# Moving where the second block's TensorE operands begin in SBUF: weight slots 8 and 16 bytes, the other buffers 128 bytes off the 256-byte lines

## The chip, the cores and the metric

The kernel runs on one core of a Trainium2 chip. The metric is the device time of one execution in microseconds (us): 2687.53 us before the change, the median of 3 runs (2683.39 to 2690.18). TensorE multiplies a moving operand, streamed from SBUF (the on-chip memory with 128 partitions), by a stationary operand that a weight load has put into the array; results go to PSUM. The other engines are VectorE (DVE), ScalarE (ACT), GpSimd (POOL) and SyncE (SP), which issues most DMAs.

## The reference, cut to what matters

Two transformer blocks run one after the other on 512 tokens of width 1024. The first block has two layers of attention and a mixture of experts; the change does not touch its arithmetic. The second block has two layers of this form:

```
h    = rms_norm_2(x, norm_mix_pre[l])
proj = h @ w_in[l]                          # 1024 -> 12 slices of 256
mix  = concat(conformer, stick-breaking attention, retention, short conv) @ w_out[l]
x    = x + rms_norm_2(mix, norm_mix_post[l])
f    = conv_ffn(rms_norm_2(x, norm_ffn_pre[l]), ffn_up[l], ffn_conv_w[l], ffn_down[l])
                                            # 1024 -> 2 x 2816, conv, silu(gate) * up, 2816 -> 1024
x    = x + rms_norm_2(f, norm_ffn_post[l])
```

All inputs are float32.

## The kernel before

In the second block every large product is made of three matmuls (`split_matmul`, lines 240 to 242): both operands are held as a high part and a low part in the type fp32r, and hi x hi, hi x lo and lo x hi are summed in one PSUM bank. Their lines in the profile are L240, L241 and L242. In a profile row `ps<-A,B` of these lines A is the moving operand and B the stationary one.

Weights come in pieces of 1 MB (128 partitions x 2048 float32): 12 pieces of `w_in`, 4 of `w_out`, 22 of `ffn_up` and 11 of `ffn_down` in each layer. SP loads a piece into one of two `raw` buffers; ACT copies it to the high part of a slot of `ring` (L2637), DVE subtracts to make the low part (L2892), and TensorE waits for `lo_made` before it uses the slot. Most pieces use the two slots `in_w` of the tile `w`; the first two pieces of `w_in` use `first`, two of `w_out` use `outs`, the second piece of `ffn_up` uses `second_up`, and `ffn_down` takes `in_w` and the halves of `h` (`in_h`) in turn, and `last_down` for its last piece.

Which operand moves depends on the product. For `w_in` and `ffn_up` the activations `h` move (512 columns, or 256 where the tokens are done in halves, `in_halves`) and the weights are stationary (128 columns); for the value slices of `w_in` it is the other way round, 256 columns of weights moving. For `w_out` and `ffn_down` 512 columns of weights move, and the mixer's outputs `y` or the feed-forward activations `act` are stationary.

Addresses: a tile `gap` before `h` makes `h`, and with it `w` and all that the planner `plan` lays behind them, begin at a multiple of 256 bytes (`LINE`). `plan.put` takes an offset in KB. So before the change `h`, both slots of `w`, `first`, `outs`, `last_down`, `act` and the `y` tiles all begin at a multiple of 256 bytes. `second_up` (at 76.3125 KB) begins 64 bytes past one. In the first block, the tile `lat_d` (1280 columns as 8 rows of 160 float32, 640 bytes apart) begins at multiples of 256 bytes and 128 past them in turn, row by row. A reader needs these three facts below.

`SECOND_AT` is where the plan of the second block's opening (`open1`, with the slots `first`) begins; it has to agree with `plan.at` (the assertion before `first = cl.split`).

The order of work on every engine is written out by hand and waits on semaphores.

Of the kernel before, what the change touches and what calls it, by code (L numbers as in the profile page):

```python
# [15 lines left out]
F32R = mybir.dt.float32r  # L16
# [4 lines left out]
P = 128  # L21
SEQ = 512
D = 1024
NT = SEQ // P
ND = D // P
# [98 lines left out]
LINE = 256  # L124


def gap_to_line(at):

    return -(-(-at // 32) * 32) % LINE
# [1293 lines left out]
    st.retire(k)  # L1423


SECOND_AT = 83 * 1024 + 768


DOWN_CUTS = (0, 256, 512, B_QR + B_KVR + B_ROPE)
# [679 lines left out]
def second_block(k, cl):  # L2109

    st = Stage(k.nc, "l")
# [1 line left out]
    par, eps, ln_eps = st.sb("par", [P, DEPTH, 3, P]), st.sb("eps", [P, 1]), st.sb("ln_eps", [P, 1])  # L2113
    ss, sd, rs = (st.sb(n, [P, 5, 2, NT]) for n in ("ss", "sd", "rs"))
    st.sb("gap", [P, gap_to_line(k.nc.sbuf_base)], mybir.dt.uint8)
    h, w = Split(st, "h", [P, ND, SEQ]), Split(st, "w", [P, 2, 2048])
    plan = Plan(k, "l", k.nc.sbuf_base)
    assert plan.at % LINE == 0

    z = [plan.put(f"z{n}", 5 * n, [P, TRI]) for n in range(2)]  # L2120
    ln1 = [plan.put(f"ln{n}", 10 + 5 * n, [P, TRI]) for n in range(2)]
# [30 lines left out]
    cm = AfterMix(st, plan, "c", 0, 84)  # L2152
    cl.lend(st, cm)

    in_w = [(w.hi[:, n, :], w.lo[:, n, :]) for n in range(2)]
    in_h = [tuple(y[:, 4 * n:4 * n + 4, :].rearrange("p a s -> p (a s)") for y in (h.hi, h.lo)) for n in range(2)]
    ring = [tuple(y[:, :] for y in x) for x in first] + [in_w[n % 2] for n in range(2, N_SLICES)]
    ring += [tuple(y[:, :] for y in x) for x in outs] + in_w
# [989 lines left out]
def program(nc, a, out):  # L3148
    k = Core(nc, a, out)
    routes = [Routes(nc, f"r{layer}") for layer in range(DEPTH)]  # L3150
    first = Stage(nc, "first")
    gap = gap_to_line(nc.sbuf_base)
    if gap:
        nc.alloc_sbuf_tensor("shared_gap", [P, gap], mybir.dt.uint8)
    base = nc.sbuf_base
    assert base % LINE == 0
    k.attention_buffers(first)
    weights = ExpertWeights(k, first)
    openings = [Collect(k, Plan(k, "open0", base), routes[0], 0, (112, 120, 128, 136), 96, 170, ((32, 40), (48, 56))),
                Collect(k, Plan(k, "open1", base + SECOND_AT), routes[1], 1, (36, 44, 68, 76), 24, 0, ((8, 52), (16, 60)))]  # L3160

    def held_first(sp):
        weights.load(sp, 0, 2, 2, lambda c: None, range(1, 2))
        weights.load_ahead(sp, 0)

    def held_second(sp):
        weights.load(sp, 1, 1, 1, lambda c: None, range(5, 6))
        weights.load_ahead(sp, 1)

    rt = window_layer(k, base, 0, routes[0], weights)  # L3170
    experts(k, 0, routes[0], rt, weights, lambda n: down_piece(k, n), held_first, openings[0])
    rt = latent_layer(k, base, 1, openings[0], routes[1], weights)
    experts(k, 1, routes[1], rt, weights, lambda n: in_piece(k, 0, n), held_second, openings[1])
    first.retire(k)
    second_block(k, openings[1])
# [24 lines left out]
```

## Time and profile before

| what | value |
|---|---|
| median of 3 runs | 2687.53 us |
| the profiled execution | 2690.91 us |
| its span, first to last instruction | 2689.1 us |
| granted TensorE clock, mean over the span | 0.974 of full speed |
| PE busy | 2505.2 us, 93% of the span |
| DVE, ACT, POOL busy | 1077.2, 754.3, 181.6 us |
| second block, from about 1496 us | granted clock 1.00, DMA share 0 to 0.47 by stage |

The second block begins at about 1496 us: its first split product starts there. A matmul's duration in the profile (0.39 us for 512 columns) contains the way through the array and overlaps the next one, so what a stream of matmuls costs is read from the distance between two starts, here called the spacing.

### The profile page before, as it was taken

To read this page: it belongs to the slowest core of one execution; us is meant where nothing else is said; L and a number is where in the kernel's file an instruction comes from. 1 tells how busy PE (TensorE), PEld (TensorE's weight loads), DVE (VectorE), ACT (ScalarE), POOL (GpSimd) and SP (SyncE) were. 2 spreads that over 40 slices of the span, in tenths; PEclk is the share of its full clock that TensorE was granted. 3 is DMA by queue.
4 is the path that set the end of the run, shared out by engine and by line. 5 is a ranking of instruction groups with operands and counts; after the bars stand their busy time and mean duration, and the time that the engine had idled before them with its cause. 6 is when DMAs were issued, how large, how long until landed. Compare 5 with 4: busy or idle time off the path is not lost.

```text
span 2689.1 us, 36859 instructions
## 1 busy us (share of the span) xinstructions
PE 2505.2 (93%) x14582; PEld 1853.1 (69%) x14582; DVE 1077.2 (40%) x1628; ACT 754.3 (28%) x1221; POOL 181.6 (7%) x302
## 2 busy tenths in 40 slices
PE   8997999888899979998888999999999999999999
PEld 7675666544576656665454777888888877888887
DVE  4753011100445541110001666655543666555542
ACT  3530000000245410000001353443332454433431
POOL 0001111111000001111111010000000010000000
PEclk9997999999999989999999999999999999999999
DMA  5339999999622189999998312223232212222231
GB/s 174 84 144 368 414 414 416 419 414 411 257 94 79 40 342 411 411 412 415 417 419 340 139 63 86 83 91 101 94 126 94 102 56 99 81 93 95 94 125 55
DMA packets 175401, 576.56 MB, mean 214 GB/s; under 512 B 20560, under 2 KB 104080, under 8 KB 125618
## 3 DMA queue, kind: packets, MB, share of 16 engines
q1 hardware_dynamic: 164722, 558.07, 53.8%
q0 software_dynamic: 10560, 16.81, 1.8%
q8 instruction: 86, 1.41, 0.2%
q14 instruction: 33, 0.27, 0.0%
HBM read 569.56 MB, written 23.07 MB: 220 GB/s over the span
## 4 chain that ended last, share of the span: by engine, by line
PE 62%; SPq 19%; DMA 3%; DVE 3%; issue 3%; ACT 2%; DVEq 0%; POOLq 0%; ACTq 0%
PE ps L240 14%; PE ps L242 14%; PE ps L241 14%; SPq L1183 13%; SPq L1189 6%; PE ps L1333 6%; PE ps L1351 4%; DMA first_weights<-in_moe_w_up 2%; PE ps L1303 1%; ACT lat_probs L1841 1%; PE ps L1650 1%; PE ps L2340 1%; PE ps L1666 1%; PE ps L2376 1%; DMA open_rows<-r_y 1%
## 5 line engine op out<-in xcount | busy, mean ns | idle before, releaser
L240 PE MATMUL ps<-l_h_hi,l_w_hi 128*128 128x512 f32 x896 | 352.9, 394 | 0.0
L241 PE MATMUL ps<-l_h_lo,l_w_hi 128*128 128x512 f32 x896 | 348.8, 389 | 0.0
L242 PE MATMUL ps<-l_h_hi,l_w_lo 128*128 128x512 f32 x896 | 348.7, 389 | 0.0
L1333 PE MATMUL ps<-first_weights,moe_xsT 128*64 128x256 f32 x2688 | 309.5, 380 | 39.6 <-DMA first_weights<-in_moe_w_up 26.9
L1412 DVE TENSOR_TENSOR moe_hid<-moe_silu,ps 128x256 f32<-128x256 f32 x64 | 27.0, 421 | 767.9 <-PE ps L1333 767.9
L1333 PEld LDWEIGHTS ps<-first_weights,moe_xsT 128*64 128x64 f32 x2688 | 225.8, 137 | 132.9 <-issue 82.7
L2892 DVE TENSOR_TENSOR l_w_lo<-l_raw,l_w_hi 128x2048 fp32r<-128x2048 f32 x76 | 174.0, 2292 | 270.1 <-ACT l_w_hi L2637 269.9
L1385 ACT ACTIVATE moe_ys<-ps 128x512 f32<-128x512 f32 x64 | 38.2, 597 | 672.3 <-PE ps L1351 672.3
L1351 PE MATMUL ps<-first_weights,moe_hidT 128*64 128x512 f32 x672 | 177.2, 675 | 38.3 <-DVE moe_hidT L1414 38.3
L2637 ACT ACTIVATE l_w_hi<-l_raw 128x2048 fp32r<-128x2048 f32 x76 | 145.2, 1914 | 179.8 <-PE ps L242 168.9
L240 PEld LDWEIGHTS ps<-l_h_hi,l_w_hi 128*128 128x128 f32 x896 | 168.2, 188 | 37.5 <-issue 2.9
L241 PEld LDWEIGHTS ps<-l_h_lo,l_w_hi 128*128 128x128 f32 x896 | 168.2, 188 | 35.4 <-issue 1.4
L242 PEld LDWEIGHTS ps<-l_h_hi,l_w_lo 128*128 128x128 f32 x896 | 168.2, 188 | 35.4
L1333 PE MATMUL ps<-first_ring,moe_xsT 128*64 128x256 f32 x1344 | 160.8, 392 | 18.4 <-DMA first_ring<-in_moe_w_up 10.0
L1333 PEld LDWEIGHTS ps<-first_ring,moe_xsT 128*64 128x64 f32 x1344 | 115.3, 141 | 67.1 <-issue 41.5
L1351 PEld LDWEIGHTS ps<-first_weights,moe_hidT 128*64 128x64 f32 x672 | 60.2, 152 | 126.3 <-issue 126.3
L1351 PE MATMUL ps<-first_ring,moe_hidT 128*64 128x512 f32 x352 | 88.9, 650 | 20.1 <-DVE moe_hidT L1414 20.1
L1291 POOL DMA_INDIRECT r_y<-moe_ys,moe_put x64 | 65.4, 1022 | 297.4 <-ACT moe_ys L1385 280.2
L1382 ACT ACTIVATE moe_silu<-ps 128x256 f32<-128x256 f32 x64 | 24.6, 384 | 214.3 <-PE ps L1333 214.3
L2956 DVE SCALAR_TENSOR_TENSOR l_gate<-l_glu,l_par,l_gate 128x512 f32<-128x512 f32 x120 | 81.8, 752 | 0.1
L240 PE MATMUL ps<-l_w_hi,l_act_hi 128*128 128x512 f32 x192 | 74.9, 390 | 0.0
L241 PE MATMUL ps<-l_w_lo,l_act_hi 128*128 128x512 f32 x192 | 74.7, 389 | 0.0
(589 smaller groups left out, 4304.2 us busy)
## 6 DMA issues: line engine op xcount, KB each, us to landing
first_weights<-in_moe_w_up SPq DMA_DIRECT2D x84, 1024.0 KB, 27.9
first_weights<-in_moe_w_down SPq DMA_DIRECT2D x84, 1024.0 KB, 27.7
first_weights<-in_moe_w_gate SPq DMA_DIRECT2D x84, 1024.0 KB, 27.4
first_ring<-in_moe_w_up SPq DMA_DIRECT2D x44, 1024.0 KB, 27.5
first_ring<-in_moe_w_down SPq DMA_DIRECT2D x44, 1024.0 KB, 27.6
l_raw<-in_ffn_up SPq DMA_DIRECT2D x44, 1024.0 KB, 5.0
first_ring<-in_moe_w_gate SPq DMA_DIRECT2D x40, 1024.0 KB, 27.6
l_raw<-in_w_in SPq DMA_DIRECT2D x22, 1024.0 KB, 4.9
```

What stands on the lines that cost most here:

```text
L240: pe.matmul(out, stationary[0], moving[0], start=first, stop=False)
L241: pe.matmul(out, stationary[0], moving[1], start=False, stop=False)
L242: return pe.matmul(out, stationary[1], moving[0], start=False, stop=last)
L1183: sp.dma_start(self.gate_up[s][m][:, 4 * c:4 * c + 4, :].rearrange("p j c -> p (j c)"), a[name][layer, e, c * 512:(c + 1) * 512, :].rearra ...
L1189: sp.dma_start(self.down[s][:, 2 * c:2 * c + 2, :].rearrange("p j c -> p (j c)"), a["moe_w_down"][layer, e, c * 256:(c + 1) * 256, :].rear ...
L1291: pool.indirect_dma_start(out=r.y_dram, out_offset=bass.IndirectOffsetOnAxis(ap=put[:, 0:1], axis=0), in_=ys[:, :], in_offset=None, bounds ...
L1333: ins = pe.matmul(k.ps[64 * h:64 * h + 64, 2 + m, 0:256], xsT[:, j, :], piece[:, j % 4, 256 * h:256 * h + 256], start=j == 0, stop=j == ND ...
L1351: ins = pe.matmul(k.ps[64 * h:64 * h + 64, 4, :], hidT[:, j % 2, 64 * (j // 2):64 * (j // 2) + 64], weights.down[s][:, j, 512 * h:512 * h ...
L1385: act.activation(ys[:, :], k.ps[:, 4, :], ACT.Copy).then_inc(ys_kept, 1)
L2637: act.activation(ring[n][0], piece(m), ACT.Copy).then_inc(hi_made, 1)
L2892: dve.tensor_tensor(lo, piece(m), hi.bitcast(F32), ALU.subtract).then_inc(lo_made, 1)
L2956: ins = dve.scalar_tensor_tensor(acc, glu[:, i, c:c + SEQ], par[:, l, 2, 2 * c + i:2 * c + i + 1], acc, ALU.mult, ALU.add)
```

## The change

Three edits. The two halves of `w` are no longer tiles of their own but views into one tile that is 128 bytes longer: slot 0 begins 2 float32 (8 bytes) past the start, slot 1 begins 4096 + 4 float32 past it (16 bytes past a multiple of 256); the low part of each begins 2048 float32 behind its high part, so it has the same 8 or 16 bytes. Because `w` is 128 bytes longer, everything in `plan` begins 128 bytes later, and so does `SECOND_AT`: `first`, `outs`, `last_down`, `act` and the `y` tiles now begin 128 bytes past a multiple of 256, and `second_up` 192. The assertion on `plan.at` goes. `h` stays where it was. The instructions of every engine, their order and their waits stay as they are; only addresses differ.

```
-SECOND_AT = 83 * 1024 + 768
+SECOND_AT = 83 * 1024 + 768 + 128
...
     st.sb("gap", [P, gap_to_line(k.nc.sbuf_base)], mybir.dt.uint8)
-    h, w = Split(st, "h", [P, ND, SEQ]), Split(st, "w", [P, 2, 2048])
+    h, w = Split(st, "h", [P, ND, SEQ]), st.sb("w", [P, 4 * 2048 + 32], F32R)
     plan = Plan(k, "l", k.nc.sbuf_base)
-    assert plan.at % LINE == 0
...
-    in_w = [(w.hi[:, n, :], w.lo[:, n, :]) for n in range(2)]
+    in_w = [tuple(w[:, at:at + 2048] for at in (past, past + 2048)) for past in (2, 4096 + 4)]
```

## Rows read from the trace of the kernel before

**Rows 1.** The page: span, and busy time of the engines.
```profile
span 2689.1 us, 36859 instructions
...
PE 2505.2 (93%) x14582; PEld 1853.1 (69%) x14582; DVE 1077.2 (40%) x1628; ACT 754.3 (28%) x1221; POOL 181.6 (7%) x302
```

**Rows 2.** Table of stretches: first block, feed-forward up-projection of layer 0.
```profile
core 0: us, PE busy (x) PEld busy (x) DVE busy (x) ACT busy (x) POOL busy (x), PEclk, DMA share, GB/s
0.00:1496.00 1496.00, 1320.98 (x8703) 878.17 (x8704) 414.78 (x892) 287.12 (x647) 158.96 (x274) 0.95 0.79 313
...
1754.00:1971.00 217.00, 217.00 (x959) 179.69 (x958) 126.90 (x140) 83.50 (x98) 0.00 (x0) 1.00 0.29 97
```

**Rows 3.** Waits of PE from 1496 us on: total, times, longest.
```profile
PE ps L2280 <- DVE l_end_xn L2908: 1.4, 1, 1.4
PE ps L2407 <- ACT l_ro L2695: 1.4, 2, 0.7
PE ps L2340 <- DVE l_wr L2979: 0.6, 2, 0.3
```

**Rows 4.** Instructions by line and shape, PE: count, busy, mean ns, idle before.
```profile
L240 PE MATMUL ps<-l_h_hi,l_w_hi 128*128 128x512 f32 x896 | 352.9, 394 | 0.0
...
L240 PE MATMUL ps<-l_w_hi,l_act_hi 128*128 128x512 f32 x192 | 74.9, 390 | 0.0
...
L240 PE MATMUL ps<-l_h_hi,l_act_hi 128*128 128x512 f32 x128 | 49.8, 389 | 0.0
...
L240 PE MATMUL ps<-l_w_hi,l_h_hi 128*128 128x256 f32 x128 | 37.7, 294 | 0.0
L240 PE MATMUL ps<-l_h_hi,open_first_hi 128*128 128x256 f32 x128 | 36.9, 289 | 0.0
...
L240 PE MATMUL ps<-l_h_hi,l_outs_hi 128*128 128x256 f32 x64 | 18.3, 286 | 0.0
L240 PE MATMUL ps<-l_h_hi,l_second_up_hi 128*128 128x256 f32 x64 | 18.1, 284 | 0.0
...
L240 PE MATMUL ps<-l_w_hi,l_y_ret 128*128 128x512 f32 x32 | 12.4, 389 | 0.0
...
L240 PE MATMUL ps<-l_last_down_hi,l_act_hi 128*128 128x512 f32 x32 | 12.4, 389 | 0.0
```

**Rows 5.** Timeline of PE, up-projection, 48 spacings apart: start, duration (us).
```profile
1760.07 0.39 PE L240 MATMUL ps<-l_h_hi,l_w_hi 128*128 128x512 f32 x1
...
1770.95 0.39 PE L240 MATMUL ps<-l_h_hi,l_w_hi 128*128 128x512 f32 x1
```

**Rows 6.** Timeline of PE, first up piece in halves, 43 spacings apart.
```profile
1729.66 0.28 PE L241 MATMUL ps<-l_h_lo,l_outs_hi 128*128 128x256 f32 x1
...
1734.82 0.28 PE L242 MATMUL ps<-l_h_hi,l_outs_lo 128*128 128x256 f32 x1
```

**Rows 7.** Timeline of PE, second up piece in halves, 18 spacings apart.
```profile
1735.77 0.28 PE L241 MATMUL ps<-l_h_lo,l_second_up_hi 128*128 128x256 f32 x1
...
1737.89 0.28 PE L241 MATMUL ps<-l_h_lo,l_second_up_hi 128*128 128x256 f32 x1
```

**Rows 8.** Timeline of PE, first block, `lat_d`: 9, then 12 spacings apart.
```profile
760.89 0.39 PE L241 MATMUL ps<-lat_x_lo,lat_d_hi 128*32 128x512 f32 x1
...
762.95 0.40 PE L241 MATMUL ps<-lat_x_lo,lat_d_hi 128*32 128x512 f32 x1
...
765.75 0.40 PE L241 MATMUL ps<-lat_x_lo,lat_d_hi 128*32 128x512 f32 x1
```

**Rows 9.** Timeline of PE, a slice of the in-projection begins: 10 spacings apart.
```profile
1524.37 0.40 PE L241 MATMUL ps<-l_h_lo,l_w_hi 128*128 128x512 f32 x1
...
1526.69 0.39 PE L242 MATMUL ps<-l_h_hi,l_w_lo 128*128 128x512 f32 x1
```

**Rows 10.** The low part of a piece on DVE: all pieces, then those of `second_up`.
```profile
L2892 DVE TENSOR_TENSOR l_w_lo<-l_raw,l_w_hi 128x2048 fp32r<-128x2048 f32 x76 | 174.0, 2292 | 270.1 <-ACT l_w_hi L2637 269.9
...
L2892 DVE TENSOR_TENSOR l_second_up_lo<-l_raw,l_second_up_hi x2: 2292/2292/2293, 1700.2 to 2293.2; 128x2048 fp32r<-128x2048 f32 x2
```

**Rows 11.** The high part of a piece on ACT: all pieces, then those of `second_up`.
```profile
L2637 ACT ACTIVATE l_w_hi<-l_raw 128x2048 fp32r<-128x2048 f32 x76 | 145.2, 1914 | 179.8 <-PE ps L242 168.9 <-DMA l_raw<-in_ffn_down 10.9
...
L2637 ACT ACTIVATE l_second_up_hi<-l_raw x2: 1918/1920/1922, 1698.3 to 2291.3; 128x2048 fp32r<-128x2048 f32 x2
```

**Rows 12.** Timeline of DVE in the up-projection: two pieces, 10.88 us apart.
```profile
1766.30 2.29 DVE L2892 TENSOR_TENSOR l_w_lo<-l_raw,l_w_hi 128x2048 fp32r<-128x2048 f32 x1 [5.62 <-ACT l_w_hi L2637]
...
1777.18 2.29 DVE L2892 TENSOR_TENSOR l_w_lo<-l_raw,l_w_hi 128x2048 fp32r<-128x2048 f32 x1 [5.70 <-ACT l_w_hi L2637]
```

## Prediction

> **What bounds the kernel now.** I read the page first, then the table of stretches, the waits, the list by line and shape, and last the timeline. The page gives TensorE 93% of the span [rows 1]. The table splits that: in the first block PE is busy for 1320.98 of 1496 us, in the up-projection of the second block for 217.00 of 217.00 us at the full clock of 2.4 GHz (1.00), with the DMA engines at 0.29 [rows 2]. From 1496 us on the list of PE's waits has three entries of together 3.4 us in about 1190 us [rows 3]. So the second block takes as long as its matmuls need to follow one another; no other engine and no transfer decides there, and a change of the spacing goes into the time one to one.
>
> The counts say what is multiplied by a spacing. Each row of [rows 4] stands for one of three equal lines (L240, L241, L242). I sort by what the edit does to the two addresses:
> A, `h` moving, `w` slots stationary: 3 x 896 = 2688.
> B, `w` moving against `act`: 3 x 192 = 576, and against the `y` tiles (`l_y_ret`, and as many for the short convolution): 2 x 3 x 32 = 192.
> C, `h` moving against `act`: 3 x 128 = 384.
> D, `w` moving over 256 columns against `h`: 3 x 128 = 384.
> E, `h` moving over 256 columns, stationary `first`, `outs`, `second_up`: 3 x (128 + 64 + 64) = 768.
> F, both operands moved by 128 bytes together, as `last_down` against `act`: their distance is unchanged, and I leave them out.
> A to E are 4992 matmuls.
>
> The spacings: 512 columns with both operands on a 256-byte line, (1770.95 - 1760.07)/48 = 0.2267 us [rows 5]; 256 columns, both on a line, (1734.82 - 1729.66)/43 = 0.1200 us [rows 6]. The difference is 106.7 ns for 256 columns, so 512 columns stream in 213.3 ns and 13.3 ns per matmul are not streaming, the same at both widths. That 13.3 ns is all that an address can win: over A to E 4992 x 13.3 = 66 us.
>
> Does the address matter at all? `second_up` is the one second-block tile that is not on a line before the change: with weights 64 bytes off, the spacing is (1737.89 - 1735.77)/18 = 0.1178 us [rows 7], 2.2 ns less than the same product from `outs` on a line [rows 6]. The weight load runs beside the matmul before it, so its address changes how long that matmul takes. The Trainium skill (SBUF — State Buffer, "Who interferes with whom") gives TensorE two independent read ports, one for the moving operand and one for the weight load; by that rule the weights' address would be worth 0 where the row shows 2.2 ns, and the trace disagrees for this type. The other way is shown too: `lat_d`, whose weight rows lie 0 and 128 bytes off in turn, takes (762.95 - 760.89)/9 = 0.2289 us and then settles at (765.75 - 762.95)/12 = 0.2333 us, 6.7 ns over the aligned stream [rows 8]. And where a stream begins, even aligned operands first wander: ten spacings take (1526.69 - 1524.37)/10 = 0.232 us [rows 9] before they are at 0.2267. So the spacing settles into one of several rhythms: 13.3 ns over streaming when aligned, 20.0 with `lat_d`, 11.0 at 64 bytes. One step between rhythms is 6.7 ns, or a third of that.
>
> **The change part by part.** It adds and removes no instruction and moves none on any queue, SP's and POOL's included; the parts are the new distances of A to E, and the writes to moved tiles.
>
> A: weights 8 or 16 bytes off, constant over the 48 matmuls of a piece. No row has such an offset. Bounds: -13.3 ns (nothing but streaming left) and +6.7 ns (the rhythm of `lat_d`), or -36 to +18 us. The nearest row is the constant 64 bytes, -2.2 ns or -6 us; the next possible one is a whole step, -6.7 ns or -18 us. The sign I take from the 64-byte row, since there too one operand stays at one distance for a whole piece. For the size I choose the whole step, because 512 columns leave the weight load twice the time of the 256-column row and so more room to fall between the reads: 2688 x 6.7 ns = 18 us.
>
> B and D: here the moving operand itself starts 8 or 16 bytes off (112 to 128 against `act` and `y`); no row shows a moving operand off the line. C and E: the weight side is 128 bytes off, which only `lat_d` has, every second row. Bounds for the 2304 matmuls as for A, -31 to +15 us; the rows nearest pull both ways (-2.2 at 64 bytes, +6.7 with `lat_d`), and I take 0. One rule speaks against B and D: the Trainium skill (SBUF — State Buffer, "Specifications (TRN2)") has 16-byte lines and a penalty for each crossing to a new one; a run of 2048 bytes that starts 8 bytes into a line touches 129 of them instead of 128. The page gives no price, and the 64-byte row cannot test it, since 64 is a whole number of lines.
>
> The writes: ACT and DVE now write `w` 8 or 16 bytes off. For `second_up`, 64 off, they take 1920 and 2292 ns against 1914 and 2292 ns on a line [rows 10, 11], so I price them at 0. Should they lengthen, DVE's gap before each low part, 5.6 us of the 10.88 us that a piece takes [rows 12], covers it; from about 5 us more per piece TensorE would wait for `lo_made`.
>
> Sum against the profiled execution: 2690.9 - 18 = 2673 us. That execution lies 3.4 us above the median of the runs (2690.9 against 2687.5), so the forecast is about 2670 us. What is late next is TensorE again, since the gap before the low parts shrinks only by 48 x 6.7 ns = 0.3 us per piece.
>
> **The rivals.**
> 1. The rhythm never settles in A (slower). With operands off the line, the stream keeps wandering as it does at its start, 0.232 us [rows 9], or as `lat_d` does on average, (765.75 - 760.89)/21 = 0.2314 us [rows 8]: about 5 ns over 0.2267. Price 2688 x 5 = 13 us, 2701; with B and D likewise 19 us, 2707. For it: alternating offsets did just that, and the two slots now differ by 8 bytes. Against: within a piece the distance is constant, and the one constant offset in the trace settled below the aligned rhythm. It decides from a mean spacing of 0.2297 us in A (8.1 us over 2688 matmuls).
> 2. Small offsets change nothing: the rhythm depends on which large part of a line is read, and 8 or 16 bytes are little beside 64. Then A and D stay, C and E are few, and the time is 2687. For it: aligned streams all settle on the same 0.2267. It is also what the rule of two ports would give.
> 3. The whole set drops a step: B to E fall as A does, 4992 x 6.7 = 33 us, 2654; two steps would be the bound of 66 us, 2621. For it: 2.2 ns were won at 256 columns as well. Against: the 128 bytes of C and E resemble the bad half of `lat_d`.
>
> **How the numbers follow.** Runs of this kernel can tell about 0.3%, or 8.1 us, from no change. The forecast has a chance of 0.40, with its own range 2660 to 2680 (a sum of -28 to -8 us; 0.02 of it lies within 0.3%); rival 3 has 0.18; rival 2 has 0.14; rival 1 has 0.28. Faster: 0.38 + 0.18 = 0.56. Within 0.3%: 0.14 + 0.02, and 0.01 of rival 1, makes 0.17. Slower: 0.27. The range runs from 2640, which holds most of rival 3 short of two steps, to 2706, nearly all of rival 1.
>
> **What would show it.** In the profile after, the 48 spacings of an up piece should span about 48 x 0.220 = 10.56 us instead of 10.88; the first block should take its 1496 us unchanged; PE's waits in the second block should stay near 3.4 us; the low parts on DVE should keep 2292 ns. A spacing of 0.2267 speaks for rival 2, of 0.230 to 0.232 for rival 1, and 256-column spacings of 0.113 with `act` products at 0.220 for rival 3. The prediction is wrong in its mechanism if the time moves by more than 8 us while the spacing in A stays at 0.2267, or if PE begins to wait.

## The result and the profile after

The median after the change is 2708.0 us (2706.9 to 2708.67, 3 runs) against 2687.53 before: a ratio of 1.0077, 95% interval 1.0059 to 1.0095. The change makes the kernel slower; the forecast of 2670 us had the wrong sign, and rival 1 had the amount (2707 us).

The page of the kernel after, span and busy times, to be held against [rows 1]:

```profile
span 2706.8 us, 36859 instructions
...
PE 2517.5 (93%) x14582; PEld 1852.3 (68%) x14582; DVE 1077.3 (40%) x1628; ACT 754.3 (28%) x1221; POOL 181.6 (7%) x302
```

The same instructions, and only PE has become busier. The span grew by 17.7 us. The table of stretches (columns as in [rows 2]) gives the first block and the up-projection of layer 0:

```profile
0.00:1494.00 1494.00, 1313.82 (x8702) 875.19 (x8703) 414.26 (x891) 287.21 (x647) 158.96 (x274) 0.96 0.79 313
1753.30:1971.00 217.70, 217.70 (x941) 176.89 (x940) 126.59 (x139) 83.12 (x98) 0.00 (x0) 1.00 0.28 93
```

The first block ends 1.5 us earlier than before (the first split product of the second block starts at 1494.82 us instead of 1496.32). In the up-projection PE is busy without a gap at the full clock, as before, but 217.70 us now hold 941 matmuls where 217.00 us held 959. The waits of PE from 1494 us on (total, times, longest) are the three of [rows 3]:

```profile
PE ps L2279 <- DVE l_end_xn L2907: 1.6, 1, 1.6
PE ps L2406 <- ACT l_ro L2694: 1.4, 2, 0.7
PE ps L2339 <- DVE l_wr L2978: 0.7, 2, 0.3
```

So no wait came in; the matmuls follow one another more slowly. PE's instructions by line and shape (count, busy, mean ns, idle before) show which, against [rows 4]; 128*128 is the shape of the stationary operand, 128x512 that of the moving one:

```profile
L240 PE MATMUL ps<-l_h_hi,l_w 128*128 128x512 f32 x896 | 356.4, 398 | 0.0
L240 PE MATMUL ps<-l_w,l_act_hi 128*128 128x512 f32 x192 | 76.0, 396 | 0.0
L240 PE MATMUL ps<-l_h_hi,l_act_hi 128*128 128x512 f32 x128 | 50.5, 395 | 0.0
L240 PE MATMUL ps<-l_w,l_h_hi 128*128 128x256 f32 x128 | 37.4, 292 | 0.0
L240 PE MATMUL ps<-l_h_hi,open_first_hi 128*128 128x256 f32 x128 | 36.8, 288 | 0.0
L240 PE MATMUL ps<-l_h_hi,l_outs_hi 128*128 128x256 f32 x64 | 18.2, 284 | 0.0
```

The three products of 512 columns rose from 394, 390 and 389 ns to 398, 396 and 395; the half-width ones fell by 1 to 2 ns. The timeline of PE in the up-projection, at the first matmul of three pieces of 48 (the first and third piece are in the slot at 8 bytes, the second in the slot at 16):

```profile
1753.32 0.39 PE L240 MATMUL ps<-l_h_hi,l_w 128*128 128x512 f32 x1
...
1764.39 0.39 PE L240 MATMUL ps<-l_h_hi,l_w 128*128 128x512 f32 x1
...
1775.59 0.39 PE L240 MATMUL ps<-l_h_hi,l_w 128*128 128x512 f32 x1
```

(1764.39 - 1753.32)/48 = 0.2306 us at 8 bytes and (1775.59 - 1764.39)/48 = 0.2333 us at 16, against 0.2267 in [rows 5]. The starts within a piece repeat: 229, 229, 234, 230, 231 ns at 8 bytes, and a cycle of six of 1400 ns at 16. The streams do settle, in longer and slower cycles.

Adding up the distances of starts in the trace by product (those across other work left out) gives the table that all experiments below are read with; A to F are the prediction's groups, "block" is the time from the first to the last split product of the second block, and every column from "block" on is in us of the profiled run.

| kernel | offsets in bytes: h / slots / plan | median | block | A | B | C | D | E | F |
|---|---|---|---|---|---|---|---|---|---|
| before | 0 / 0 / 0 | 2687.5 | 1186.9 | 609.1 | 173.0 | 87.0 | 46.3 | 92.1 | 64.8 |
| after | 0 / 8, 16 / 128 | 2708.0 | 1206.2 | 621.4 | 177.7 | 89.2 | 45.8 | 91.4 | 65.4 |
| plan_only | 0 / 0 / 128 | 2696.5 | 1193.7 | 609.3 | 177.5 | 89.2 | 46.2 | 91.5 | 65.0 |
| slots_only | 0 / 8, 16 / 0 | 2706.5 | 1204.7 | 621.7 | 177.5 | 87.1 | 45.8 | 92.1 | 65.1 |
| both_8 | 0 / 8, 8 / 128 | 2704.7 | 1204.8 | 619.1 | 178.0 | 89.2 | 46.2 | 91.3 | 65.4 |
| all_128 | 128 / 128 / 128 | 2686.8 | 1186.9 | 609.3 | 173.0 | 87.0 | 46.3 | 92.1 | 64.8 |
| h_minus_4 | -4 / 0 / 0 | 2697.0 | 1195.7 | 618.9 | 173.0 | 87.1 | 46.3 | 90.5 | 64.8 |
| w_minus_4 | 0 / -4 / 0 | 2702.6 | 1203.2 | 625.5 | 173.0 | 87.1 | 45.7 | 92.0 | 65.0 |
| hw_minus_4 | -4 / -4 / 0 | 2693.0 | 1191.6 | 615.1 | 173.0 | 87.1 | 45.5 | 90.8 | 65.1 |

After against before: A +12.3, B +4.7, C +2.2, D -0.5, E -0.7, F +0.6, together 18.6 of the block's 19.3 us. The block is a steadier measure than the median: the first block, whose work is the same in all nine kernels, took from 1483 to 1491 us in the profiled runs (first matmul to the first split product of the second block), while before and all_128 have the same 1186.9 us for the second.

### The profile page after: what moved, and what is told of

Same layout as the page of the kernel before. It is cut to its first block, busy times and chain, and to the rows that moved or that the text cites. A ratio compares the mean times of both kernels' runs of the same rounds, so it can differ in the third digit from the quotient of the medians.

```text
span 2706.8 us, 36859 instructions
## 1 busy us (share of the span) xinstructions
PE 2517.5 (93%) x14582; PEld 1852.3 (68%) x14582; DVE 1077.3 (40%) x1628; ACT 754.3 (28%) x1221; POOL 181.6 (7%) x302
## 4 chain that ended last, share of the span: by engine, by line
PE 70%; SPq 18%; DMA 4%; DVE 3%; issue 3%; ACT 2%; DVEq 0%; POOLq 0%; ACTq 0%
PE ps L240 16%; PE ps L241 16%; PE ps L242 16%; SPq L1183 11%; PE ps L1333 7%; SPq L1189 6%; PE ps L1351 4%; DMA first_ring<-in_moe_w_up 1%; PE ps L1303 1%; DMA first_weights<-in_moe_w_up 1%; ACT lat_probs L1841 1%; PE ps L1650 1%; PE ps L2339 1%; PE ps L1666 1%; DMA r_x<-resid 1%
## 5 line engine op out<-in xcount | busy, mean ns | idle before, releaser
L240 PE MATMUL ps<-l_h_hi,l_w 128*128 128x512 f32 x896 | 356.4, 398 | 0.0
L241 PE MATMUL ps<-l_h_lo,l_w 128*128 128x512 f32 x896 | 353.4, 394 | 0.0
L242 PE MATMUL ps<-l_h_hi,l_w 128*128 128x512 f32 x896 | 352.6, 394 | 0.0
L2891 DVE TENSOR_TENSOR l_w<-l_raw,l_w 128x2048 fp32r<-128x2048 f32 x76 | 174.1, 2292 | 283.9 <-ACT l_w L2636 283.9
L1351 PE MATMUL ps<-first_weights,moe_hidT 128*64 128x512 f32 x672 | 170.4, 652 | 38.4 <-DVE moe_hidT L1414 38.4
L2636 ACT ACTIVATE l_w<-l_raw 128x2048 fp32r<-128x2048 f32 x76 | 145.3, 1914 | 192.6 <-PE ps L242 181.8
L240 PEld LDWEIGHTS ps<-l_h_hi,l_w 128*128 128x128 f32 x896 | 169.7, 189 | 41.9 <-issue 2.9
L242 PEld LDWEIGHTS ps<-l_h_hi,l_w 128*128 128x128 f32 x896 | 168.1, 188 | 38.9
L241 PEld LDWEIGHTS ps<-l_h_lo,l_w 128*128 128x128 f32 x896 | 168.5, 188 | 37.8 <-issue 1.4
L1351 PE MATMUL ps<-first_ring,moe_hidT 128*64 128x512 f32 x352 | 92.3, 671 | 20.1 <-DVE moe_hidT L1414 20.1
L1291 POOL DMA_INDIRECT r_y<-moe_ys,moe_put x64 | 65.4, 1022 | 294.2 <-ACT moe_ys L1385 275.2
L1382 ACT ACTIVATE moe_silu<-ps 128x256 f32<-128x256 f32 x64 | 24.6, 384 | 216.2 <-PE ps L1333 216.2
L1351 PEld LDWEIGHTS ps<-first_ring,moe_hidT 128*64 128x64 f32 x352 | 31.4, 151 | 65.7 <-issue 65.7
L240 PE MATMUL ps<-l_w,l_act_hi 128*128 128x512 f32 x192 | 76.0, 396 | 0.0
```

Of the source, the lines that this page charges most:

```text
L240: pe.matmul(out, stationary[0], moving[0], start=first, stop=False)
L241: pe.matmul(out, stationary[0], moving[1], start=False, stop=False)
L242: return pe.matmul(out, stationary[1], moving[0], start=False, stop=last)
L1291: pool.indirect_dma_start(out=r.y_dram, out_offset=bass.IndirectOffsetOnAxis(ap=put[:, 0:1], axis=0), in_=ys[:, :], in_offset=None, bounds ...
L1351: ins = pe.matmul(k.ps[64 * h:64 * h + 64, 4, :], hidT[:, j % 2, 64 * (j // 2):64 * (j // 2) + 64], weights.down[s][:, j, 512 * h:512 * h ...
L2636: act.activation(ring[n][0], piece(m), ACT.Copy).then_inc(hi_made, 1)
```

## The experiments

Three theories stood against each other. Theory 1: a product's spacing depends on the distance between its two operands within the 256-byte line. Theory 2: on the weights' own offset. Theory 3: on the change from 8 to 16 bytes between pieces. They are told apart by streams at constant offsets, and by undoing one part of the change at a time.

**sweep.** What does an offset cost by itself?

```
GROUPS = [(512, 0, 0)] * 4 + [(512, 0, d) for d in range(0, 256, 4)]     # columns, moving at, stationary at
GROUPS += [(512, d, 0) for d in range(0, 256, 8)] + [(512, d, d) for d in range(0, 256, 32)] + [(256, 0, d) for d in range(0, 256, 8)]
...
pe.matmul(ps[g % 8][:, 0:cols], base_st[:, to:to + 128], base_mv[:, fro:fro + cols], ...)   # 97 per group
```

> A measurement by itself: only the load and store of x, and 140 streams of 97 matmuls each (fp32r, 128 x 128 weights, new weights for every matmul) are left of the program; nothing else is computed. Each stream keeps both operands at one offset past a 256-byte line: 512 moving columns with the weights 0 to 252 bytes off in steps of 4; 512 columns with the moving operand 0 to 248 off; both off together; 256 columns with the weights 0 to 248 off. Theory 1 (the spacing depends on the distance between the two operands within the line): weights at 0 give 226.7 ns, at 8 about 230.7, at 16 about 233.3, at 128 about 232; the moving operand at d gives what the weights give at 256 - d; both together give 226.7 at every offset. Theory 2 (the weights' own offset counts, whatever the moving operand's): the moving operand alone gives 226.7 everywhere, and both together give what the weights alone give. Theory 3 (a constant offset costs nothing once the stream has settled; what costs is the change from 8 to 16 bytes between pieces): every stream of 512 columns settles at 226.7.

The timeline of PE (start, time from the first start to the last end, count). The last matmul's own 0.39 us (0.28 for 256 columns, as in [rows 6]) has to be taken off, and 96 spacings remain. Here are weights at 0, 4, 8, 16, 64, 128 and 252 bytes; then the moving operand alone at 8 and 128; both at 64 and at 128; and 256 columns with weights at 0, 8 and 64:

```profile
102.97 22.16 PE L45 MATMUL ps_e<-base_mv,base_st 128*128 128x512 f32 x97
124.96 22.71 PE L45 MATMUL ps_f<-base_mv,base_st 128*128 128x512 f32 x97
147.51 22.54 PE L45 MATMUL ps_g<-base_mv,base_st 128*128 128x512 f32 x97
...
192.20 22.79 PE L45 MATMUL ps_a<-base_mv,base_st 128*128 128x512 f32 x97
...
463.20 22.79 PE L45 MATMUL ps_e<-base_mv,base_st 128*128 128x512 f32 x97
...
824.00 22.71 PE L45 MATMUL ps_e<-base_mv,base_st 128*128 128x512 f32 x97
...
1521.93 22.15 PE L45 MATMUL ps_d<-base_mv,base_st 128*128 128x512 f32 x97
...
1565.93 22.80 PE L45 MATMUL ps_f<-base_mv,base_st 128*128 128x512 f32 x97
...
1905.24 22.79 PE L45 MATMUL ps_e<-base_mv,base_st 128*128 128x512 f32 x97
...
2312.86 22.18 PE L45 MATMUL ps_g<-base_mv,base_st 128*128 128x512 f32 x97
...
2356.90 22.18 PE L45 MATMUL ps_a<-base_mv,base_st 128*128 128x512 f32 x97
...
2444.98 11.78 PE L45 MATMUL ps_e<-base_mv,base_st 128*128 128x256 f32 x97
2456.60 11.38 PE L45 MATMUL ps_f<-base_mv,base_st 128*128 128x256 f32 x97
...
2537.03 11.16 PE L45 MATMUL ps_e<-base_mv,base_st 128*128 128x256 f32 x97
```

The settled spacings (mean of the last 48 of each stream) are: 226.7 ns on the line; 232.4, 230.6, 233.3, 233.3, 232.4 and 226.7 ns for the six weight offsets; 233.3 for the moving operand at 8 and at 128; 226.7 for both operands at one offset, at all seven tried. Over the 63 weight offsets no spacing is below 226.7; five equal it (120, 132, 144, 156 and 252), 28 are at 233.3, the highest at 237. The 8 and 16 bytes that slowed A in the kernel cost the same here, alone and constant, so theory 3 falls. Theory 2 falls by the moving operand alone and by both together. Of theory 1 the first and the last part hold; its mirror (the moving operand at d is as the weights at 256 - d) does not: only 11 of 31 pairs agree within 0.15 ns. Each offset was run from one start only; what that leaves open is the question of the run phase below.

At 256 columns it is the other way round: 120.0 ns on the line, below that at 24 of 31 offsets, 115.6 at 8 and 113.3 at 64. The same 64 bytes thus win 6.7 ns at 256 columns and lose 6.7 ns at 512.

**plan_only, slots_only, both_8.** Each part of the change by itself, and the slots alike.

```
 plan_only   -    ... for past in (2, 4096 + 4)]
             +    ... for past in (0, 4096)]
 slots_only  -SECOND_AT = 83 * 1024 + 768 + 128        -st.sb("w", [P, 4 * 2048 + 32], F32R)
             +SECOND_AT = 83 * 1024 + 768 + 256        +st.sb("w", [P, 4 * 2048 + 64], F32R)
             -plan.put("conv", 90.5, ...)              -plan.put(f"end_xn{n}", 90.5 + 4 * n, ...)
             +plan.put("conv", 90.375, ...)            +plan.put(f"end_xn{n}", 90.375 + 4 * n, ...)
 both_8      -    ... for past in (2, 4096 + 4)]
             +    ... for past in (2, 4096 + 2)]
```

> The weight slots begin on the line again, the plan stays 128 bytes off. Theories 1 and 2: the products of h with the slots go back to 226.7 ns (12.2 us less than after the change); act and the y tiles as weights stay 128 off and keep about 232 ns against h and against the slots (2.2 + 4.5 us over before), so about 2694 us. Theory 3: nothing alternates any more, 2687 to 2689 us.

> The weight slots keep 8 and 16 bytes, the plan begins on a line again (256 bytes later than before; two small buffers that are no TensorE operands are 128 bytes lower so that it fits). Products of h with the slots: 233 ns as after the change (+12.2 us); h against act back at 226.7. Slots moving against act and y, all of these on the line: theory 1 gives them the distance of 8 or 16 bytes the other way round, 768 x about 5 ns = 4 us, so 2703 to 2704 us; theory 2 gives them 226.7 again, so 2700 us. Theory 3: the alternation is all there, 2704 us or more.

> As after the change, but both slots begin 8 bytes off. Theories 1 and 2: the half of the products of h that ran at 233.3 ns runs at 230.7, 1344 x 2.7 = 3.6 us less than after the change, about 2704 us. Theory 3: the slots no longer differ, so what is left over before is the plan's 128 bytes alone, at most 2694 us.

Measured: plan_only 2696.5 us, ratio 1.0028 (1.0017 to 1.0039); slots_only 2706.5, 1.0063 (1.0049 to 1.0077); both_8 2704.7, 1.0070 (1.0056 to 1.0084). By line and shape, plan_only:

```profile
L240 PE MATMUL ps<-l_h_hi,l_w 128*128 128x512 f32 x896 | 352.9, 394 | 0.0
L240 PE MATMUL ps<-l_w,l_act_hi 128*128 128x512 f32 x192 | 75.9, 395 | 0.0
L240 PE MATMUL ps<-l_h_hi,l_act_hi 128*128 128x512 f32 x128 | 50.5, 395 | 0.0
```

and slots_only:

```profile
L240 PE MATMUL ps<-l_h_hi,l_w 128*128 128x512 f32 x896 | 356.8, 398 | 0.0
L240 PE MATMUL ps<-l_w,l_act_hi 128*128 128x512 f32 x192 | 76.0, 396 | 0.0
L240 PE MATMUL ps<-l_h_hi,l_act_hi 128*128 128x512 f32 x128 | 49.9, 390 | 0.0
```

The slots carry A (394 or 398 ns), the plan carries C (395 or 390), and either of them alone is enough for all of B. Against before, plan_only costs 6.8 us of block time and slots_only 17.8; the two make 24.6, and less the 4.5 us of B that both contain, 20.1, against 19.3 for the whole change. In slots_only the weights of B lie on the line and only the moving operand is off, and B costs as much, which theory 2 excludes. In both_8 nothing alternates any more and A falls by just 2.3 of its 12.3 us, in the direction of the difference between the two slots' rhythms, though less than the 3.6 us that I had worked out from it; theory 3 falls here too.

**sweep_order.** The first sweep again, in the kernel's order of addresses.

```
q, j, term = n // 24, n // 3 % 8, n % 3
to = s // 4 + 2048 * (term == 2) + 256 * j + 128 * (q % 2)
fro = 4096 * (term == 1) + 512 * j + (256 * (q // 2 % 2) if cols == 256 else 0)
```

> A second measurement by itself (load and store of x and 132 streams of 97 matmuls are left, nothing else is computed): now in the order and with the steps of the kernel's up-projection (high x high, low x high, high x low; weights 1024 and 8192 bytes apart, the moving operand 2048 and 16384), moving operand on the line, weights 0 to 252 bytes off, for 256 and for 512 columns. In the first sweep 64 bytes gave 113.3 ns at 256 columns, in the kernel 117.7 (l_second_up). Theory 1 (only the distance within the 256-byte line counts, whatever the steps): the same spacings as in the first sweep, 113.3 at 64 and 88 bytes, 115.6 at 8, 120.0 at 0. Rival (the rhythm also depends on the order or on larger steps, or on what ran before): 117.7 at 64, and other offsets are the best ones. By both, no offset at 512 columns comes below 226.7, and most lie near 233.3.

At 512 columns every one of the 64 spacings came out as in the first sweep within 0.1 ns. At 256 columns 26 of the 32 offsets common to both repeated within 0.3 ns (113.3 at 64 and 88, 115.5 at 8), and six did not (208 bytes: 116.7 then, 120.0 now; 232: 123.3 and 117.8). The kernel's own 117.8 at 64 bytes [rows 7] stayed unexplained, so something beside the distance had a say.

**all_128, h_minus_4, w_minus_4.** The map taken back to the kernel.

```
 all_128    -st.sb("gap", [P, gap_to_line(k.nc.sbuf_base)], ...)     (and SECOND_AT + 128)
            +st.sb("gap", [P, gap_to_line(k.nc.sbuf_base) + 128], ...)
 h_minus_4  -h, w = Split(st, "h", [P, ND, SEQ]), Split(st, "w", [P, 2, 2048])
            +h, w = Shifted(st.sb("h", [P, 2 * 4096 + 8], F32R), 7), Split(st, "w", [P, 2, 2048])    # gap - 32
 w_minus_4  +w, h = st.sb("w", [P, 4 * 2048 + 8], F32R), Split(st, "h", [P, ND, SEQ])                # gap - 32
            +in_w = [... for past in (7, 4096 + 7)]
```

> The kernel before with everything of the second block, h included, 128 bytes later: every operand is off its 256-byte line, no two operands change their distance. Theory 1 (distance): 2687 us as before, products of h with the slots at a mean of 228.5 ns, act products at 226.7 to 227. Theory 2 (the weights' own offset): what 128 bytes cost act and y in plan_only (5.8 ns) on all 3840 products of 512 columns, 22 us, so about 2709 us.

> The kernel before with h 4 bytes earlier, all else on the line: slots and act begin 4 bytes after the moving h. From the sweep at weights 4 bytes behind (232.4 ns against 226.7): (2688 + 384) x 5.7 = 17.6 us slower; the 768 half-width products at 118.3 instead of 120.0 give back about 1 us; slots against act stay at 226.7. About 2687 + 16.5 = 2703.5 us, ratio 1.0062. A rival by which the size of the offset counts and not its sign expects the same of this kernel and the next one.

> The kernel before with the slots of w 4 bytes earlier (w lies ahead of h for that), all else on the line: the slots begin 4 bytes before the moving h, 252 past a line. The sweep has 226.7 ns at 252 bytes: products of h with the slots stay where they were, h against act too. Slots moving against act and y see the weights 4 bytes behind: 768 x 5.7 = 4.4 us slower; half-width slots against h 384 x 1.7 = 0.6 us faster. About 2687 + 3.8 = 2691 us, ratio 1.0014. By the rival in which only the size of the offset counts, 2688 x 5.7 = 15 us slower at least, 2703 us or more.

all_128 took 2686.8 us, ratio 0.9995 (0.9986 to 1.0004), with the products of before, by line and shape:

```profile
L240 PE MATMUL ps<-l_h_hi,l_w_hi 128*128 128x512 f32 x896 | 353.0, 394 | 0.0
L240 PE MATMUL ps<-l_w_hi,l_act_hi 128*128 128x512 f32 x192 | 74.9, 390 | 0.0
```

Every operand is 128 bytes off and nothing is lost: it is the distance between the two operands that the 128 bytes of the change spoiled. The other two were misses. h_minus_4 took 2697.0 us, 1.0035 (1.0021 to 1.0049), and w_minus_4 2702.6, 1.0055 (1.0041 to 1.0069). In h_minus_4 act lies 4 bytes behind the moving h exactly as the slots do, and pays nothing:

```profile
L240 PE MATMUL ps<-l_h,l_w_hi 128*128 128x512 f32 x896 | 355.0, 396 | 0.0
...
L240 PE MATMUL ps<-l_h,l_act_hi 128*128 128x512 f32 x128 | 49.7, 388 | 0.0
```

and in w_minus_4 the slots 252 bytes on settle at (1772.65 - 1761.45)/48 = 0.2333 us (mean of A 234.6 ns), where the sweep had 226.7:

```profile
1761.45 0.40 PE L240 MATMUL ps<-l_h_hi,l_w 128*128 128x512 f32 x1
...
1772.65 0.40 PE L240 MATMUL ps<-l_h_hi,l_w 128*128 128x512 f32 x1
```

The two kernels differ (232.1 and 234.6 ns), so the size of the offset alone is refuted as well. Part of the miss of h_minus_4 was in my sum: I held a settled 232.4 against a settled 226.7, but the mean of A in the kernel before is 228.5 with the wandering at its starts, and only 232.1 - 228.5 = 3.7 ns remained as the loss.

**phase.** Does the start decide?

```
stream(g, 512, 0, 16)       # aligned
stream(g, lead, 0, 1)       # 256 to 270 columns
stream(g, cols, s, N)       # 61 matmuls at the offset
```

> A third measurement by itself (load and store of x and the streams are left, nothing else is computed), on why the sweeps give 232.4 and 226.7 ns at 4 and 252 bytes while in h_minus_4 and w_minus_4 the act products at 4 bytes stayed at 226.8 and the products of h with the slots at 252 bytes took 233.3. Each stream of 61 matmuls in the kernel's order has one distance (0, 4, 8, 16, 64, 128 or 252 bytes) and 512 or 256 columns; ahead of it run 16 aligned matmuls of 512 columns, and then one of 256 to 270 columns in steps of 2, which shifts where in the rhythm the stream begins. Theory 1a (a distance allows several rhythms, and the start decides which one a stream falls into): at 4 and 252 bytes some starts settle at 226.7 and others at 230 to 233.3, at 64 bytes with 256 columns some at 113.3 and others at 117.8, while distance 0 settles at 226.7 from every start. Rival (the distance alone decides, and it is something else in the kernel, such as the larger distance between the buffers, that made the difference): all eight starts of a distance settle at the same spacing, 226.7 at 252 and 232.4 at 4.

The timeline of PE; each row is the last aligned matmul, the lead and the stream of 61. First 512 columns at 252 bytes behind leads of 256 and of 258 columns, then 256 columns at 64 bytes behind the same two leads:

```profile
952.89 14.34 PE L46 MATMUL ps_e<-base_mv,base_st 128*128 128x512 f32 x63
...
970.48 14.74 PE L46 MATMUL ps_f<-base_mv,base_st 128*128 128x512 f32 x63
...
1446.85 7.42 PE L46 MATMUL ps_e<-base_mv,base_st 128*128 128x512 f32 x63
...
1457.53 7.69 PE L46 MATMUL ps_f<-base_mv,base_st 128*128 128x512 f32 x63
```

Two columns more in one matmul ahead make the stream 0.40 us longer: 0.40/60 = 6.7 ns per spacing. Of the eight starts, at 252 bytes three settle at 226.7 and five at 233.3; at 64 bytes with 256 columns two at 113.3 and six at 117.8, which is the kernel's figure for `second_up` [rows 7]; at 16 bytes one at 226.7 and seven at 233.3. At distance 0 every start settles at 226.7 (120.0 at 256 columns), at 8 bytes every one at 230.7. Theory 1a holds for 252, 16 and, at 256 columns, 64 bytes, but 4 bytes gave 232.3 from all eight starts, so the act products stayed open. Open, too, is why the kernel's own starts pick the rhythm they do: in w_minus_4 all 44 pieces of A whose second half runs without other work in between settled at 233.3.

**down_order.** What do the act products have that the slots do not?

```
"up":   to, fro = 256 * (trio % 8) + 128 * (trio // 8 % 2), 512 * (trio % 8)
"down": to, fro = 512 * (2 * (trio // 16) + trio % 2) + 128 * (trio // 4 % 4), 1024 * (trio % 2) + 512 * (trio // 2 % 2)
```

> A fourth measurement by itself (load and store of x and the streams are left), on what is left over: in h_minus_4 act lay 4 bytes behind the moving h, and in w_minus_4 behind the moving slots, and both ran at 226.8 to 227.1 ns, while slots 4 bytes behind h took 232.1, and 4 bytes took 232.3 from every start in the last run. Streams of 97 matmuls of 512 columns at four offsets (weights 4 bytes on; moving operand 252 on; moving operand 248 on; weights 128 on), in the order of addresses of the up-projection or of the down-projection, with 24 or 6 matmuls per PSUM bank, the low weights 8 or 44 KB behind the high ones, and started without a lead or with one of 256 or 262 columns. Theory 1 as it stands (distance and start): 232.3 at 4 bytes in all eight combinations, 230.7 at 8, 232.4 or 233.3 at 128. Rival: one of the three settings that act differs in brings 4 bytes to 226.7 while 128 stays at 232 or more; the combinations show which. If none does, it is something that the kernel has beside these streams.

The timeline of PE, moving operand 252 on, 24 matmuls in each row (23 spacings, and 0.39 us for the last); two rows in the up-projection's order, then two in the down-projection's:

```profile
774.89 5.70 PE L52 MATMUL ps_f<-base_mv,base_st 128*128 128x512 f32 x24
780.42 5.69 PE L52 MATMUL ps_g<-base_mv,base_st 128*128 128x512 f32 x24
...
1087.81 5.60 PE L52 MATMUL ps_b<-base_mv,base_st 128*128 128x512 f32 x24
1093.25 5.60 PE L52 MATMUL ps_c<-base_mv,base_st 128*128 128x512 f32 x24
```

The first two rows are 230.9 and 230.4 ns by this, the last two 226.5: the same operands in the down-projection's order. Over the whole streams: 230.6 against 226.7 ns, from all three starts; the number of matmuls per bank and the distance of the low weights change nothing (0.1 ns). So the order of addresses made the difference for act; and A in h_minus_4, in the up-projection's order with `h` moving 252 on, settles at 230.5 ns in the kernel, as these streams do, and not at the 232.4 of the sweep's weights 4 on. With the weights 4 or 128 bytes on instead, both orders take 232.4 to 232.5 ns; distance alone is therefore not all, since weights 4 on and moving operand 252 on are the same distance.

**hw_minus_4.** The one layout that these maps left as a possible winner.

```
+hw = st.sb("hw", [P, 2 * 4096 + 4 * 2048 + 8], F32R)
+h = Shifted(hw, 7)
+in_w = [tuple(hw[:, at:at + 2048] for at in (past, past + 2048)) for past in (7 + 8192, 7 + 8192 + 4096)]
```

> The kernel before with h and the slots 4 bytes earlier together, act, y, first, outs and second_up where they were: the one layout seen so far that should keep every 512-column product at its floor and take something off the half-width ones. Products of h with the slots: distance 0, 228.5 ns mean as before. Slots and h moving (252 on) against act and y: by h_minus_4, w_minus_4 and the last run's down-projection order 226.7 to 227.1, nothing lost; by distance alone 232.3, 960 x 5.6 = 5.4 us lost. Half-width products of h: 118.8 and 117.6 ns as in h_minus_4, 1.7 us less than before. Sum 2686 us, ratio 0.9994, too little to tell from no change in the times, but to be seen in the spacings; by distance alone 2691 us, ratio 1.0014.

It took 2693.0 us, ratio 1.0020 (1.0011 to 1.0030): slower. B, C and E came as forecast (173.0, 87.1 and 90.8 us), but A took 615.1 us, a mean of 230.7 ns a product against 228.5 before, though the distance of its two operands is 0. In the up-projection a piece takes (1762.70 - 1751.70)/48 = 0.2292 us per matmul, against 0.2267 in [rows 5] (`h` and the slots are one tile here, so the row has one name for both operands):

```profile
1751.70 0.39 PE L240 MATMUL ps<-l_hw 128*128 128x512 f32 x1
...
1762.70 0.39 PE L240 MATMUL ps<-l_hw 128*128 128x512 f32 x1
```

The zero distances that kept the floor were multiples of 32 bytes; one that begins 4 bytes before a line did not. No layout that was run beats the kernel before.

## Why the prediction was wrong

- *What bounds the kernel*: right. PE's waits in the second block stayed at 3.7 us, the first block took its time unchanged (1494.82 against 1496.32 us), and the change of spacing went into the time one to one (18.6 us of the sum in 19.3 of the block).
- *The failed step* is the one on A: "The sign I take from the 64-byte row, since there too one operand stays at one distance for a whole piece". That row has 256 columns [rows 7], A has 512. The sweep shows that the sign turns with the width: 64 bytes take 6.7 ns off at 256 columns and add 6.7 at 512. On the line, 512 columns are already at the lowest of all offsets tried, while 256 columns are among the highest. So A, put at -18 us, measured +12.3, and my reason for the size (more room for the weight load at 512 columns) is shown by no run: every spacing below that of the line was at 256 columns.
- *The bound* "13.3 ns is all that an address can win" was never in reach for 512 columns, where no settled spacing below 226.7 ns appeared in any run. (The rhythm at 64 bytes is 117.8 - 106.7 = 11.1 ns over streaming, not 11.0.) The upper bound, the 6.7 ns of `lat_d` [rows 8], was the right end and the right row: it has 512 columns. I used it only as the end of a range. It was no true bound either: single offsets of the sweep reach 237.0 ns (weights 164 bytes on) and 240.0 (moving operand 88 on), 10 and 13 ns over the line. And its stationary operand has 32 columns (128*32 in [rows 8]), not the 128 of A, which I did not weigh.
- *B to E at 0*: with `act` and `y` at 128 bytes and the slots at 8 and 16, the distances in B are 120 and 112 bytes, not "112 to 128". B measured +4.7 and C +2.2, D -0.5 and E -0.7 us, together +5.7, inside my bounds of -31 to +15. The two rows that "pull both ways" were of different width, and each was right for its own width.
- *F* left out: +0.6 us, and 0.0 in all_128.
- *The writes at 0*: right. The low parts of the slots on DVE keep their 2292 ns and the high parts on ACT their 1914. Here are the low parts, and two of them in the up-projection, 11.19 us apart where [rows 12] have 10.88:

```profile
L2891 DVE TENSOR_TENSOR l_w<-l_raw,l_w 128x2048 fp32r<-128x2048 f32 x76 | 174.1, 2292 | 283.9 <-ACT l_w L2636 283.9
```

```profile
1766.54 2.29 DVE L2891 TENSOR_TENSOR l_w<-l_raw,l_w 128x2048 fp32r<-128x2048 f32 x1 [5.78 <-ACT l_w L2636]
1777.73 2.29 DVE L2891 TENSOR_TENSOR l_w<-l_raw,l_w 128x2048 fp32r<-128x2048 f32 x1 [6.01 <-ACT l_w L2636]
```

- *Rival 1* had A's and B's sign and, at 2707 us, the time; my range ended at 2706, below that. Its mechanism was wrong: the streams do not wander on, they settle in cycles of five and six matmuls whose mean is 230.7 and 233.3 ns. That the total came so close is in part luck: it had D slower, where D measured -0.5 us, and left out C, which measured +2.2. Rival 2 (small offsets are little) fell: 8 bytes cost as much as 128 to within 2 ns. Rival 3 held in sign for 256 columns only.
- *The two rules of the Trainium skill.* The two independent read ports (SBUF — State Buffer, "Who interferes with whom") would leave the spacing at 226.7 ns wherever the weights lie; the sweep has up to 237 ns by moving the weights alone, so for these fp32r streams the measurement decides against it. For the 16-byte lines (same page, "Specifications (TRN2)") no price appeared by itself: the moving operand 32 or 128 bytes off, a whole number of such lines, costs 6.7 ns like 8 bytes. Nor does a start inside such a line cost anything by itself: with the moving operand 252 bytes on, C and B of hw_minus_4 kept 226.8 and 227.0 ns, and with the weights 252 on three of eight starts in phase kept 226.7. So this rule does not explain A's 230.7 ns in hw_minus_4, which stays open.

What stays open is the mechanism behind the spacing. The runs show that the two operands' places in the line set it, with width, order and start; they do not show through what.

## What to carry to other kernels

Where matmuls follow one another without a gap, read the spacing for each width apart: a price taken at 256 columns had the opposite sign at 512. Keep the moving and the stationary operand of long fp32r streams of 512 columns at the same offset from a 256-byte line, in steps of 32 bytes; such a common offset itself cost nothing here, while with one of 252 bytes A took 2.2 ns more per product. Before a layout is changed for some bytes, a sweep of streams at all offsets costs one run and shows whether the place taken now is already the floor. It is not enough to choose another place: the sweep's 226.7 ns at 252 bytes became 233.3 in the kernel, because order and start count as well.

## What the runs showed that I had not expected

- One stream can run in two settled rhythms and keep the one it fell into: at 252 bytes 226.7 or 233.3 ns, chosen by two columns of one matmul before it. With both operands on the line all eight starts ended in the same rhythm.
- The order of addresses alone moved a spacing by 3.9 ns (230.6 to 226.7 with the moving operand 252 on).
- 256 columns came down to 113.3 ns, 6.7 over streaming at the 213.3/2 = 106.7 of the prediction's sum; 512 columns never came below 13.3 over streaming.
